# A two-layer transformer pair on one core: gather, row parts, router order and GpSimd's place in the expert stages

## The chip, the cores and the metric

The program runs on one core of a Trainium2 chip. The metric is the device time of one execution in microseconds (us); the time of a kernel is the median of its runs. Engines are called PE (TensorE), PEld (its weight loads), DVE (VectorE), ACT (ScalarE), POOL (GpSimd) and SP (SyncE, which here only issues DMAs).

## The reference, cut to what matters

256 tokens of width 1024 pass through a first block (block attention, a short convolution, two dense feed-forward parts) and a second one (a gated recurrence, a stick-breaking attention, two expert parts). The change is in the two expert parts, each of which computes this, with 4 groups of 4 experts of width 256:

```python
probs_g = softmax(xf @ w_group + b_group)              # 4 groups
p_top, g_idx = top_k(probs_g, 1)                       # every token takes one group
logits_e = (xf @ w_router + b_router).reshape(T, 4, 4)
w_top, e_local = top_k(softmax(logits_e[group]), 2)    # and two experts in it
gates = p_top * w_top / sum(w_top) at those two experts
h = silu(xf @ w_gate[e]) * (xf @ w_up[e])
y = sum over e of gates[:, e] * (h @ w_down[e])
```

All is float32. Matrix products are made of three products of parts: a float32 value is cut into a high part (a copy rounded to the type that PE multiplies at full rate) and a low part (value minus high part), and high*high, high*low and low*high are summed.

## The kernel before, in words

**Weights.** All weights are streamed in units of 1 MB (128 partitions x 2048 float32). SP loads a unit into one of 6 raw buffers, ACT writes its high part (`split`, line 678), DVE its low part (line 1347), PE multiplies with it, each engine in the same order of units, with 3 buffers of parts. A raw buffer is loaded again when both parts of its unit are written. Before a stage, `ahead` splits its first three units.

**Sorting tokens by group.** An expert stage (`moe`, once as "moe0" and once as "moe1") sorts the 256 tokens into four windows of 128 slots, one for each group, and a fifth one for what doesn't fit, so that the matrices of an expert meet one window only. In the order of time:

- After the norm, PE transposes the rows x (`after_norm`, line 2691); ACT and DVE apply the gain and bias of the norm and write the high and low part `h_high` and `h_low` in four blocks of two columns k (lines 749 and 1442).
- `router` (lines 2704 and 2705): 32 small products give the router's sums; first all eight k of token tile 0, then all of tile 1. Ahead of it and of other waits PE runs `keep_busy`: products of no use, so many calls (two instructions of the trace each) that it isn't idle.
- DVE adds biases and finds each token's group (lines 1910 to 1926); it signals `group_ready` at line 1924. PE counts tokens with triangular products (line 2729, `pos_ready`), DVE turns the counts into places and writes two selection matrices of 128 x 512 (line 1935, `sel_ready`, counted twice for each stage) into `act_high` and `act_low`.
- ACT writes the high part of the un-transposed rows (line 1135), once the router's products are done, since it lies in the same memory as `h_high`; DVE writes its low part (line 1939) into the memory of `h_low`.
- PE gathers (line 2743): for each of the 8 column blocks k, rows times selection matrix gives the transposed tokens of all four windows, 512 columns in one PSUM bank; 32 products. The banks are `GBANK`, two of them used twice. ACT takes each bank out with gain and bias (line 1143, 128 x 512) into `in_windows`, and window 0 gets its high part (line 1154, in two halves) and low part from DVE (line 2015, in two halves, `window_ready`).
- Meanwhile DVE copies the selection matrices for later use (line 1942), finds the base of the overflow group (lines 1944 to 1958), and ranks the experts (`ranks`, lines 1964 to 1975: 15 instructions of at most 40 elements), and only then comes its first half of window 0; the gates follow (`gates`, lines 1981 to 1999), then the second half.

**The expert loop.** 20 tiles c, four experts on each of the four windows and four on the fifth. `gate_up(c)`: 24 products of 512 columns (two units); in tile 0 PE also makes the gates of the slots between the two halves (`gate_in`, line 2759). ACT takes the silu (line 1160), DVE the product with the gate (line 2022), PE turns it (`turn`, line 2804), ACT and DVE write its parts (lines 1166 and 2029), and `down(c)` follows with a third unit, after `gate_up(c + 1)`. For `sel_turn` (line 2769) PE transposes the selection matrices after tile 0; `scatter` brings windows back to rows.

**GpSimd.** `apply_rows` multiplies the rows x by the norm's gain and adds its bias in place, four instructions of 128 x 1024 with a wait between any two (lines 645 and 647). They must come after the last reading of the bare rows. Before, in the expert stages, they wait for `window_ready`: both halves of window 0. After them POOL issues DMAs for later rows of constants. The rows that it writes are next read for the overflow window, after tile 2 (`over_in`, which waits for `ln_applied`).

Of the kernel before, what the change touches and what calls it, by code (L numbers as in the profile page):

```python
# [10 lines left out]
ALU = mybir.AluOpType  # L11
# [84 lines left out]
GBANK = (0, 1, 4, 5, 6, 7, 4, 5)  # L96
# [4 lines left out]
def build(nc, A, out):  # L101
    ctx = ExitStack()
    with ctx:
# [17 lines left out]
        tv = sb("rows", [P, TT, D])  # L121
        W = sb("scratch", [P, 41 * 256])
        Z = sb("small", [P, 8 * 256])
# [39 lines left out]
        rows_h, rows_l = (a[:, :, :].rearrange("p k (t s) -> p k t s", t=TT) for a in (hh, hl))  # L163
# [235 lines left out]
        def half_heads(u):  # L399

            return slice(3 * u, 3 * u + 3)

# [174 lines left out]
        def _(pool):  # L577
# [59 lines left out]
            def apply_rows(turns):  # L637
# [3 lines left out]
                if turns != 8:  # L641
                    pool.wait_ge(window_ready, 2 if turns == 7 else GRP + 4)
# [18 lines left out]
        def _(act):  # L661
# [464 lines left out]
            sp_in, rsum, rhi = Count(router_ready), Count(router_sums), Count(rows_high)  # L1126
# [4 lines left out]
            def moe(ph, scale, shift):  # L1131
                def sort_in():

                    act.wait_ge(router_sums, rsum.up())
# [6 lines left out]
                    for k in range(KT):  # L1141
                        act.wait_ge(gathered, gth.up())
                        act.activation(in_windows[:, 0:GRP, k, :], ps[:, GBANK[k], :].rearrange("p (w s) -> p w s", w=GRP),
                                       ACT.Identity, bias=shift[:, k:k + 1], scale=scale[:, k:k + 1]).then_inc(gather_taken, 1)
                        gtk.up()
# [187 lines left out]
        def _(dve):  # L1333
# [572 lines left out]
            def sort_in():  # L1906
# [21 lines left out]

                place, over = by_tile(rt[:, 304:312]), rt[:, 312:314]
# [81 lines left out]
            def moe(ph):  # L2011
# [122 lines left out]
        def _(pe):  # L2134
# [546 lines left out]
            def after_norm(count, fill):  # L2681
                keep_busy(fill, 0)
                for t in range(TT):
# [4 lines left out]
                    for g in range(4):  # L2688
# [3 lines left out]
                        if t:  # L2692
                            i.then_inc(xt_ready, 1)
                            xt.up()

            def router():

                keep_busy(8, 0)
                pe.wait_ge(rw_low, rwlr.up())
                for t in range(TT):  # L2700
                    tok = slice(t * P, (t + 1) * P)
                    for k in range(KT):
                        bank_of_h(t == 0, k)
                        pe.matmul(ps[:, 3, 40 * t:40 * t + 40], hh[:, k, tok], rwr[:, k, :], start=k == 0, stop=False, skip_group_check=True)
# [11 lines left out]
            def moe(applied):  # L2716
                first_tri, all_ones = mstrict[:, 0:P], ones[:, :]

                def sort_in():
# [3 lines left out]
                    pe.matmul(ps[:, 2, 0:P], all_ones, ident[:, :], start=False, stop=True, skip_group_check=True)  # L2723
                    pe.wait_ge(group_ready, grp.up())
# [10 lines left out]
                    for k0 in (0, 4):  # L2735
                        for part in (rows_h, rows_l):
                            if part is rows_l and k0 == 0:
                                pe.wait_ge(rows_low, rlo.up())
                            for k in range(k0, k0 + 4):
                                if part is rows_h and k >= 6:  # L2740
                                    pe.wait_ge(gather_taken, gtk.value(k - 3))
                                for t in range(TT):
                                    i = pe.matmul(ps[:, GBANK[k], :], part[:, k, t, :], sel_r[t],  # L2743
# [239 lines left out]
```

## Time and profile before

| | |
|---|---|
| median of 3 runs | 1465.17 us (1461.89 to 1466.07) |
| the profiled execution's own time | 1463.39 us |
| span of its trace | 1461.7 us |
| mean granted clock of PE, share of full | 0.971 |
| PE busy | 1367.6 us, 94% of the span |
| PEld busy | 1170.8 us, 80% |
| DVE busy | 1037.7 us, 71% |
| ACT busy | 767.4 us, 52% |
| POOL busy | 88.4 us, 6% |
| DMA | 327.72 MB, mean 224 GB/s |

The trace is of one execution. Busy shares are means over stages that have different limits; what a part of the change is worth has to be read in its own stage. A row of the timeline has the start in us from the start of the span, the duration in us of one instruction or of several in a row, the engine, the line, the operation, what it writes and reads, how many, and in brackets the idle time of the engine before it with what ended it. The first expert stage begins with the norm at about 869 us and its loop ends at about 1097; the second goes from about 1222 to 1447, some 352.7 us later.

### The profile page before, as it was taken

The page shows a single profiled execution, that of the slowest core. Times are in us where ns is not written, and L with a number is a line of the kernel's source. Part 1 is how long each engine was busy: PE and PEld are TensorE (multiplying, and loading weights), DVE is VectorE, ACT ScalarE, POOL GpSimd, SP SyncE. Part 2 cuts the span into 40 slices and gives each one's busy share as a digit, 9 for nine tenths or more (in the row PEclk, how much of TensorE's full clock was granted, in tenths as well). Part 3 has the DMA queues.
Part 4 walks back from the last instruction along what each step waited for, and adds up shares of the span by engine and source line. Part 5 has one row for each costly group of instructions (what it writes and reads, how often), then busy time and mean ns, then how long its engine had stood idle before and what let it go on. Part 6 is the DMA issues. An engine that isn't in the chain of part 4 may idle for free.

```text
span 1461.7 us, 19477 instructions
## 1 busy us (share of the span) xinstructions
PE 1367.6 (94%) x7482; PEld 1170.8 (80%) x7482; DVE 1037.7 (71%) x1057; ACT 767.4 (52%) x753; POOL 88.4 (6%) x81
## 2 busy tenths in 40 slices
PE   5996889999999999999999988999998988999995
PEld 5975778888799878888999977888878977788884
DVE  6686677788776566454665757788885465888886
ACT  2666343434433343433465345677774565577773
POOL 0010000000000000000000012200004000400000
PEclk9999899999999999999999998999998999899998
DMA  9984558999585366555553341999994413499991
GB/s 358 387 303 156 174 174 300 309 309 307 185 285 172 114 204 203 187 188 174 171 159 130 112 134 59 311 330 349 348 355 134 161 59 113 121 345 348 347 355 41
DMA packets 208909, 327.72 MB, mean 224 GB/s; under 512 B 9456, under 2 KB 146352, under 8 KB 208832
## 3 DMA queue, kind: packets, MB, share of 16 engines
q1 hardware_dynamic: 195536, 276.71, 56.5%
q0 software_dynamic: 13296, 49.93, 10.3%
q8 instruction: 54, 0.88, 0.3%
q14 instruction: 23, 0.19, 0.0%
HBM read 325.56 MB, written 1.05 MB: 223 GB/s over the span
## 4 chain that ended last, share of the span: by engine, by line
PE 79%; DVE 12%; ACT 5%; issue 2%; DMA 1%; SPq 0%; DVEq 0%; ACTq 0%
PE ps L2140 23%; PE ps L2142 22%; PE ps L2141 22%; DVE w_low L1347 3%; ACT w_high L678 2%; PE ps L2639 1%; PE ps L2837 1%; PE ps L2743 1%; PE ps L2481 1%; DMA raw<-in_w_qkv 1%; DVE stats L1861 1%; DVE h_low L2015 1%; DVE x_rows L1852 1%; DVE ps L1453 1%; PE ps L2804 1%
## 5 line engine op out<-in xcount | busy, mean ns | idle before, releaser
L1347 DVE TENSOR_TENSOR w_low<-raw,w_high 128x2048 fp32r<-128x2048 f32 x254 | 588.2, 2320 | 268.8 <-ACT w_high L678 266.7
L678 ACT ACTIVATE w_high<-raw 128x2048 fp32r<-128x2048 f32 x254 | 484.1, 1908 | 344.8 <-PE ps L2142 317.6
L2140 PE MATMUL ps<-w_high,h_high 128*128 128x512 f32 (+1 forms) x896 | 355.6, 397 | 11.4 <-DVE h_low L1442 4.0
L2142 PE MATMUL ps<-w_high,h_low 128*128 128x512 f32 (+1 forms) x896 | 348.2, 389 | 0.0
L2141 PE MATMUL ps<-w_low,h_high 128*128 128x512 f32 (+1 forms) x896 | 347.9, 388 | 0.0
L2140 PEld LDWEIGHTS ps<-w_high,h_high 128*128 128x128 f32 x896 | 170.1, 190 | 46.5 <-issue 8.2
L2142 PEld LDWEIGHTS ps<-w_high,h_low 128*128 128x128 f32 x896 | 169.6, 189 | 35.1
L2141 PEld LDWEIGHTS ps<-w_low,h_high 128*128 128x128 f32 x896 | 170.3, 190 | 32.4 <-issue 0.2
L2140 PE MATMUL ps<-h_high,w_high 128*128 128x256 f32 x592 | 172.3, 291 | 5.2 <-DVE h_low L1442 3.8
L2141 PE MATMUL ps<-h_low,w_high 128*128 128x256 f32 x592 | 169.3, 286 | 0.0
L2142 PE MATMUL ps<-h_high,w_low 128*128 128x256 f32 x592 | 169.2, 286 | 0.0
L2140 PE MATMUL ps<-w_high,act_high 128*128 128x512 f32 x336 | 133.5, 397 | 4.4 <-DVE act_low L2029 4.4
L2142 PE MATMUL ps<-w_high,act_low 128*128 128x512 f32 x336 | 131.1, 390 | 0.0
L2141 PE MATMUL ps<-w_low,act_high 128*128 128x512 f32 x336 | 130.9, 390 | 0.0
L2140 PEld LDWEIGHTS ps<-h_high,w_high 128*128 128x128 f32 x592 | 115.5, 195 | 8.9 <-issue 8.6
L2141 PEld LDWEIGHTS ps<-h_low,w_high 128*128 128x128 f32 x592 | 115.5, 195 | 0.5 <-issue 0.5
L2142 PEld LDWEIGHTS ps<-h_high,w_low 128*128 128x128 f32 x592 | 115.4, 195 | 0.0
L2140 PEld LDWEIGHTS ps<-w_high,act_high 128*128 128x128 f32 x336 | 63.1, 188 | 24.1 <-DVE act_low L2029 10.7
L2142 PEld LDWEIGHTS ps<-w_high,act_low 128*128 128x128 f32 x336 | 63.1, 188 | 13.4
L2141 PEld LDWEIGHTS ps<-w_low,act_high 128*128 128x128 f32 x336 | 63.1, 188 | 12.4
L586 POOL DMA_DIRECT2D scratch<-in_w_ada x40 | 30.2, 755 | 471.9 <-DVE scratch L1395 264.9
L1395 DVE SCALAR_TENSOR_TENSOR scratch<-scratch,silu_c 128x512 f32<-128x512 f32 x70 | 52.6, 752 | 2.5
(352 smaller groups left out, 1483.6 us busy)
## 6 DMA issues: line engine op xcount, KB each, us to landing
raw<-in_w_down SPq DMA_DIRECT2D x124, 512.0 KB, 5.0
raw<-in_w_gate_up SPq DMA_DIRECT2D x88, 512.0 KB, 5.2
scratch<-in_w_ada POOLq DMA_DIRECT2D x40, 1024.0 KB, 5.6
raw<-in_w_gate SPq DMA_DIRECT2D x80, 512.0 KB, 5.2
raw<-in_w_up SPq DMA_DIRECT2D x80, 512.0 KB, 6.8
raw<-in_w_qkv SPq DMA_DIRECT2D x24, 512.0 KB, 13.0
raw<-in_w_o SPq DMA_DIRECT2D x24, 512.0 KB, 4.8
raw<-in_w_in SPq DMA_DIRECT2D x24, 512.0 KB, 4.9
```

The costliest lines, as they stand in the source:

```text
L586: pool.dma_start(cring[:, q, :, :], v[:, q * UK:(q + 1) * UK, bass.ds(c * NC, NC)]) \
L678: act.activation(wh[u % SPL][:, :, 0:w], raw[u % RAW][:, :, 0:w], ACT.Copy).then_inc(h_split, 1)
L1347: dve.tensor_tensor(wl[u % SPL][:, :, 0:w], raw[u % RAW][:, :, 0:w], wh[u % SPL][:, :, 0:w].bitcast(F32), ALU.subtract).then_inc(l_split, 1)
L1395: i = dve.scalar_tensor_tensor(acc, w, s, acc, ALU.mult, ALU.add)
L1453: dve.tensor_scalar(b, b, scale[:, k:k + 1], shift[:, k:k + 1], ALU.mult, ALU.add).then_inc(v_ready if q else dve_step, 1)
L1852: dve.scalar_tensor_tensor(x2, x2, ALPHA, ps[:, 4 + 2 * t:6 + 2 * t, :], ALU.mult, ALU.add).then_inc(dve_step, 1)
L1861: dve.bn_stats(st[:, 32 + 12 * t + 6 * a:38 + 12 * t + 6 * a], xs[:, t, a * 512:(a + 1) * 512]).then_inc(dve_step, 1)
L2015: dve.tensor_tensor(window_h(hl, w)[:, ks, :], in_windows[:, w, ks, :], window_h(hh, w)[:, ks, :].bitcast(F32), ALU.subtract).then_inc(win ...
L2140: pe.matmul(o, h1, h2, start=start, stop=False, skip_group_check=True)
L2141: pe.matmul(o, h1, l2, start=False, stop=False, skip_group_check=True)
L2142: return pe.matmul(o, l1, h2, start=False, stop=stop, skip_group_check=True)
L2481: i = pe.transpose(ps[:, 2, k * S + t * P:k * S + (t + 1) * P], Z[:, 512 + t * FW + k * P:512 + t * FW + (k + 1) * P], ident[:, :])
```

## The change

In both expert stages:

1. The high part of the rows lies in the memory of `rows` and the low part in two pieces of `features` and `scratch`, no longer over `h_high` and `h_low`. ACT writes the high part without waiting for the router's sums. DVE writes the low part in two instructions, and ahead of its wait for PE's counts (`pos_ready`) instead of behind the selection matrices.
2. The gather is made in two halves: windows 0 and 1 for all k ahead of `gate_up(0)` (32 products of 256 columns), windows 2 and 3 (32 more) in the new `other_windows` behind `gate_up(0)`, ahead of `turn`. Each bank holds two k, and ACT takes out 128 x 256 eight times ahead of the loop and eight times after the first silu. To make room for these, the high and low part of the unit of `down(0)` are written in tile 1, ahead of that tile's own.
3. The router's products go block by block (k outside, tiles inside).
4. POOL's four instructions wait for the selection matrices (`sel_ready`), no longer for window 0.
5. More `keep_busy`: 14 calls for 10 after the norm, 3 new ones between the transposes of the two token tiles (also in the stage after moe0, which has the same function), 11 for 8 ahead of the router, 5 new ones ahead of the wait for `group_ready`.

The diff, without the declarations of memory:

```diff
@@ gpsimd, apply_rows
                 if turns != 8:
-                    pool.wait_ge(window_ready, 2 if turns == 7 else GRP + 4)
+                    pool.wait_ge(sel_ready, 2 if turns == 7 else 4)
@@ scalar, moe
+                def windows_out(w0, k):
+                    if k % 2 == 0:
+                        act.wait_ge(gathered, gth.up())
+                    act.activation(in_windows[:, w0:w0 + 2, k, :], gather_bank(k).rearrange("p (w s) -> p w s", w=2),
+                                   ACT.Identity, bias=shift[:, k:k + 1], scale=scale[:, k:k + 1]).then_inc(gather_taken, 1)
                 def sort_in():
-                    act.wait_ge(router_sums, rsum.up())
                     act.activation(rows_h, x_parts, ACT.Copy).then_inc(rows_high, 1)
...
                     for k in range(KT):
-                        act.wait_ge(gathered, gth.up())
-                        act.activation(in_windows[:, 0:GRP, k, :], ps[:, GBANK[k], :].rearrange("p (w s) -> p w s", w=GRP),
-                                       ACT.Identity, bias=shift[:, k:k + 1], scale=scale[:, k:k + 1]).then_inc(gather_taken, 1)
+                        windows_out(0, k)
...
                 split()
                 silu()
-                split(1, True)
+                for k in range(KT):
+                    windows_out(2, k)
                 n[0] += 2
                 for c in range(1, NTILE):
                     w, e = divmod(c, GRP)
                     high()
+                    if c == 1:
+                        split(-1, True)
                     split()
@@ vector, sort_in
+                dve.wait_ge(rows_high, rhi.up())
+                for i, x in enumerate(rows_l):
+                    ks = slice(UK * i, UK * i + UK)
+                    dve.tensor_tensor(x, x_parts[:, ks, :, :], rows_h[:, ks, :, :].bitcast(F32), ALU.subtract).then_inc(rows_low, 1)
+                    dve.wait_ge(rows_low, rlo.up())
                 dve.wait_ge(pos_ready, psr.up())
...
-                dve.wait_ge(rows_high, rhi.up())
-                dve.tensor_tensor(rows_l, x_parts, rows_h.bitcast(F32), ALU.subtract).then_inc(rows_low, 1)
-                dve.wait_ge(rows_low, rlo.up())
@@ vector, moe
                 product(0)
-                split(1)
                 n[0] += 2
                 for c in range(1, NTILE):
                     w, e = divmod(c, GRP)
                     low_part()
+                    if c == 1:
+                        split(-1)
                     split()
@@ tensor, after_norm, router, moe
                             xt.up()
+                    if t == 0:
+                        keep_busy(3, 0)
...
-                keep_busy(8, 0)
+                keep_busy(11, 0)
                 pe.wait_ge(rw_low, rwlr.up())
-                for t in range(TT):
-                    tok = slice(t * P, (t + 1) * P)
-                    for k in range(KT):
-                        bank_of_h(t == 0, k)
-                        pe.matmul(ps[:, 3, 40 * t:40 * t + 40], hh[:, k, tok], rwr[:, k, :], start=k == 0, ...)
+                for k in range(KT):
+                    bank_of_h(True, k)
+                    for t in range(TT):
+                        tok = slice(t * P, (t + 1) * P)
+                        pe.matmul(ps[:, 3, 40 * t:40 * t + 40], hh[:, k, tok], rwr[:, k, :], start=k == t == 0, ...)
...
+                    keep_busy(5, 0)
                     pe.wait_ge(group_ready, grp.up())
...
+                def gather(k, w0, low):
+                    part = rows_l[k // UK][:, k % UK] if low else rows_h[:, k]
+                    for t in range(TT):
+                        i = pe.matmul(gather_bank(k), part[:, t, :], sel_r[t][:, w0 * P:(w0 + 2) * P], ...)
+                    if low and k % 2:
+                        i.then_inc(gathered, 1)
+
+                def other_windows():
+                    pe.wait_ge(gather_taken, gtk.up(KT))
+                    for k in range(0, KT, 2):
+                        for low in (False, True):
+                            for j in range(2):
+                                gather(k + j, 2, low)
...
                 def sel_turn():
+                    pe.wait_ge(gather_taken, gtk.up(KT))
...
                 sort_in()
                 gate_up(0)
+                other_windows()
...
-            after_norm(5, 10)
+            after_norm(5, 14)
...
-            after_norm(7, 10)
+            after_norm(7, 14)
```

## Rows read from the trace of the kernel before

**Rows 1.** The page's chain of work that ended last, shares by engine.

```profile
PE 79%; DVE 12%; ACT 5%; issue 2%; DMA 1%; SPq 0%; DVEq 0%; ACTq 0%
```

**Rows 2.** Waits from 905 to 1100 us: waiting instruction, who ended it, total, times, longest.

```profile
ACT w_high L678 <- PE ps L2142: 29.1, 26, 3.8
```

**Rows 3.** Timeline of PE at the entry of the first expert stage.

```profile
878.17 1.95 PE L2226 MATMUL ps<-ident,ones 128*128 128x128 f32 x16
880.98 0.26 PE L2704 MATMUL ps<-router_parts,h_high 128*128 128x40 f32 x1 [0.85 <-DVE h_low L1442]
...
887.58 0.37 PE L2705 MATMUL ps<-router_parts,h_low 128*128 128x20 f32 x1
...
893.56 0.80 PE L2743 MATMUL ps<-act_high,h_high 128*128 128x512 f32 x1
...
902.33 0.40 PE L2743 MATMUL ps<-act_low,h_low 128*128 128x512 f32 x1
902.57 0.40 PE L2140 MATMUL ps<-w_high,h_high 128*128 128x512 f32 x1
...
905.67 2.41 PE L2759 MATMUL ps<-gates,scratch 128*128 128x4 f32 x20 [0.21 <-DVE h_low L2015]
...
913.09 0.69 PE L2804 MATMUL ps<-ident,small 128*128 128x128 f32 x2 [2.13 <-DVE small L2022]
...
920.42 0.39 PE L2140 MATMUL ps<-w_high,act_high 128*128 128x512 f32 x1
```

**Rows 4.** Timeline of DVE in the same stretch.

```profile
883.11 2.28 DVE L1347 TENSOR_TENSOR w_low<-raw,w_high 128x2048 fp32r<-128x2048 f32 x1
887.98 0.20 DVE L1910 TENSOR_TENSOR scratch<-ps,scratch 128x40 f32<-128x40 f32 x1 [2.59 <-PE ps L2705]
...
889.27 0.17 DVE L1924 TENSOR_TENSOR scratch<-scratch 128x8 f32<-128x8 f32 x1
...
892.82 0.69 DVE L1935 TENSOR_TENSOR act_low<-ps,scratch 128x512 fp32r<-128x512 f32 x1
...
895.87 0.43 DVE L1942 COPY scratch<-act_high 128x512 f32<-128x512 f32 x1
...
898.35 0.09 DVE L1964 MEMSET scratch<- 128x40 f32 x1
...
901.65 0.69 DVE L2015 TENSOR_TENSOR h_low<-features,h_high 128x512 fp32r<-128x512 f32 x1
...
904.93 0.69 DVE L2015 TENSOR_TENSOR h_low<-features,h_high 128x512 fp32r<-128x512 f32 x1 [0.48 <-ACT h_high L1154]
```

**Rows 5.** Timeline of ACT in the same stretch.

```profile
887.98 1.91 ACT L1135 ACTIVATE h_high<-x_rows 128x2048 fp32r<-128x2048 f32 x1 [3.82 <-PE ps L2705]
...
901.38 2.78 ACT L1143 ACTIVATE features<-ps,cols 128x512 f32<-128x512 f32 x4 [0.63 <-PE ps L2743]
```

**Rows 6.** Timeline of POOL, its instructions in the first expert stage.

```profile
905.86 4.21 POOL L645 TENSOR_TENSOR x_rows<-x_rows,scratch 128x1024 f32<-128x1024 f32 x1 [47.91 <-DVE h_low L2015]
910.15 4.29 POOL L647 TENSOR_TENSOR x_rows<-x_rows,scratch 128x1024 f32<-128x1024 f32 x1
...
918.95 2.41 POOL L647 TENSOR_TENSOR x_rows<-x_rows,scratch 128x1024 f32<-128x1024 f32 x1
```

**Rows 7.** Timeline of DVE beside those instructions of POOL.

```profile
907.74 4.48 DVE L1347 TENSOR_TENSOR w_low<-raw,w_high 128x2048 fp32r<-128x2048 f32 x1
...
912.15 0.16 DVE L2006 COPY scratch<-ps 128x16 f32<-128x16 f32 x1
...
919.91 3.59 DVE L1347 TENSOR_TENSOR w_low<-raw,w_high 128x2048 fp32r<-128x2048 f32 x1 [2.98 <-ACT w_high L678]
```

**Rows 8.** Stretches: length, busy us of PE, PEld, DVE, ACT, POOL, granted clock, DMA share, GB/s.

```profile
913.20:916.40 3.20, 3.20 (x9) 2.62 (x10) 3.19 (x1) 0.38 (x1) 3.12 (x2) 0.50 0.79 246
```

**Rows 9.** Timeline of PE in the second expert stage.

```profile
1271.83 0.39 PE L2140 MATMUL ps<-w_high,act_high 128*128 128x512 f32 x1
```

**Rows 10.** Timeline of PE in the stage after the first expert stage.

```profile
1104.65 1.97 PE L2691 MATMUL ps<-ident,x_rows 128*128 128x128 f32 x8 [0.77 <-DVE x_rows L1880]
```

More of the change, by code:

```diff
@@ L121, in build @@
         tv = sb("rows", [P, TT, D])
+        rows_at = nc.sbuf_base - TT * D * 4
+        rows_hi = nc.alloc_sbuf_tensor_at("rows_high_part", [P, KT, S], F32R, offset=rows_at)
         W = sb("scratch", [P, 41 * 256])
+        scratch_at = nc.sbuf_base - 41 * 256 * 4
+        rows_lo = [nc.alloc_sbuf_tensor_at(f"rows_low_part{i}", [P, UK, S], F32R, offset=o)
+                   for i, o in enumerate((features_at + 16 * S * 4, scratch_at + 20 * 256 * 4))]
         Z = sb("small", [P, 8 * 256])
@@ L161, in build @@
         rt = W[:, 12 * 256:20 * 256]
-        rows_h, rows_l = (a[:, :, :].rearrange("p k (t s) -> p k t s", t=TT) for a in (hh, hl))
+        rows_h = rows_hi[:, :, :].rearrange("p k (t s) -> p k t s", t=TT)
+        rows_l = [a[:, :, :].rearrange("p k (t s) -> p k t s", t=TT) for a in rows_lo]
         x_parts = xs[:, :, :].rearrange("p t (k s) -> p k t s", s=P)
@@ L401, in half_heads, with gather_bank @@
             return slice(3 * u, 3 * u + 3)
+        def gather_bank(k):
+            return ps[:, 4 + k // 2, (k % 2) * S:(k % 2 + 1) * S]
         def level_bank(l, u):
@@ L1125, in _ @@
             transposed_mod(*ln_cols(0, 0), 0)
-            sp_in, rsum, rhi = Count(router_ready), Count(router_sums), Count(rows_high)
+            sp_in, rhi = Count(router_ready), Count(rows_high)
             gth, gtk, whi = Count(gathered), Count(gather_taken), Count(window_high)
@@ L2734, in sort_in @@
                     pe.wait_ge(rows_high, rhi.up())
-                    for k0 in (0, 4):
-                        for part in (rows_h, rows_l):
-                            if part is rows_l and k0 == 0:
+                    for k0 in (0, UK):
+                        for low in (False, True):
+                            if low:
                                 pe.wait_ge(rows_low, rlo.up())
[L2739 to L2743, printed above, removed]
-                                                  start=part is rows_h and t == 0, stop=part is rows_l and t == 1, skip_group_check=True)
-                                if part is rows_l:
-                                    i.then_inc(gathered, 1)
-                                    gth.up()
-                    gtk.up(8)
+                            for k in range(k0, k0 + UK):
+                                gather(k, 0, low)
+                def gather(k, w0, low):
+                    part = rows_l[k // UK][:, k % UK] if low else rows_h[:, k]
+                    for t in range(TT):
+                        i = pe.matmul(gather_bank(k), part[:, t, :], sel_r[t][:, w0 * P:(w0 + 2) * P],
+                                      start=not low and t == 0 and k % 2 == 0, stop=low and t == 1, skip_group_check=True)
+                    if low and k % 2:
+                        i.then_inc(gathered, 1)
+                        gth.up()
+                def other_windows():
+                    pe.wait_ge(gather_taken, gtk.up(KT))
+                    for k in range(0, KT, 2):
+                        for low in (False, True):
+                            for j in range(2):
+                                gather(k + j, 2, low)
                 def gate_in():
```

5 lines of the change are left out of this document (2 added, 3 removed).

## The prediction

> **What bounds the kernel now.** I read the chain of work that ended last first: PE has 79% of it, DVE 12%, ACT 5% [rows 1]. Then the waits in the first expert loop: the weight copies of ACT wait for PE to free buffers, 29.1 us in 26 waits, and none in the list waits for a raw load [rows 2]. So the loop runs at PE's pace, and what the change can move is the time at which the loop gets under way; a microsecond won or lost ahead of tile 1 is carried to the end, twice (moe0 and moe1). So the timelines of the engines from 869 to 925 us are the view that decides. There the path is: PE's router until 887.9, slowed by a clock that has fallen to half on the way (its first product has 0.26 us, its last 0.37) [rows 3]; DVE's selection until 893.5 [rows 4]; PE's gather from 893.56 to 902.57, when `gate_up(0)` starts [rows 3]. DVE's ranks end at 901.6, and the low part of window 0 ends at 902.3 [rows 4], so DVE is as late as the gather: taking time from the gather alone brings next to nothing. Then PE idles 2.13 us ahead of `turn(0)` at 913.09, because DVE's product is late [rows 3], and after this idle time the clock is at half for 3.2 us [rows 8], which costs 1.6. `down(0)` starts at 920.42.
>
> **The router and the row parts.** A call of `keep_busy` takes 0.24 us at full clock (16 instructions, 8 calls, in 1.95) [rows 3]. The idle time of PE ahead of the router, 0.85 us [rows 3], is filled by 3 calls, that ahead of the second transposes, about the same (0.77 in the later stage) [rows 10], by 3 more; they just fit. If the clock stays full, 32 products at the pace of the fills or a little under, 0.11 us, are 3.5 us from 880.98: the router ends at about 884.5, 3.4 earlier. But DVE then still has a weight split, until 885.39 [rows 4], so its chain starts at 885.4 for 887.98. `group_ready` comes 1.46 later (887.98 to 889.44) [rows 4], at 886.9. ACT's high part of the rows, 1.91 us [rows 5], no longer waits and is done by 886.1. The low part, 2.3 us in one instruction, some 2.5 in two, now stands where DVE waited 2.2 us for the counts: from 887.1 to 889.6. PE's ten counting products, 1.1 to 2.3 us after 886.9, are hidden beside it. Place and selections take 1.7 us: done at 891.3, for 893.5 before. **Gain 2.2 us**, and no wait for the low part is left in the gather. The 5 new calls ahead of `group_ready` end at 886.3 at full clock; at half clock they would be 1.1 us late, which the low part hides.
>
> **The gather.** A product of 512 columns takes 0.24 us at full clock (902.33 to 902.57) [rows 3], so 32 of 256 columns, at 0.12, are 3.8 us: 891.3 to 895.2. ACT's takings, 0.70 for 512 columns [rows 5], so about 0.43 for 256, end near 897. By themselves they would let the loop start at 897. What holds it is DVE: from the copy at 895.87 to the window at 901.65 it has 5.8 us of work [rows 4], in the new kernel from 891.3 to 897.1, then the window's 0.7. Without GpSimd PE would start `gate_up(0)` at 897.8, 4.8 us earlier than before.
>
> **GpSimd.** Its four instructions now start at 891.5, in the middle of this work. What do they do to DVE? Beside DVE's weight splits the trace shows it: the split that was issued at 907.74 lasted 4.48 us, where an undisturbed one has 2.28 [rows 4, 7]; POOL's first instruction ended at 910.07 (905.86 + 4.21) [rows 6], and 910.07 + 2.2 is 912.2, the split's end. The one issued at 919.91 lasted 3.59 us [rows 7]: POOL's last one, which ran already, ended at 921.36 at its own pace of 2.41 [rows 6], and 921.36 + 2.2 is 923.5 again. So two instructions don't share the time; the later one stands until the other ends. And the copy from PSUM at 912.15 took 0.16 [rows 7] while POOL's second instruction was waiting or running (910.15 to 914.44) [rows 6]: an instruction that reads PSUM isn't held.
>
> This rule is also in the Trainium skill, page "SBUF — State Buffer", section "Who interferes with whom": DVE instructions with two inputs in SBUF, and copies in a two-port mode, exclude a GpSimd instruction that reads SBUF for the whole of either. It speaks against this part of the change; this case's trace agrees for large instructions, and no run here shows it yet for small ones. With shared bandwidth instead, the sum below would be that of the second rival.
>
> No row shows small DVE instructions of two SBUF inputs beside POOL. The lower bound of their cost is nothing; the upper one is four holds of 2.3 us, 9.2. The nearest rows are the held splits, of the same operation, so I take the hold for small ones too. Then: the first copy runs (891.3 to 891.7), POOL takes its turn to 894.0, the second copy, POOL to 896.6, one instruction or two, POOL to 899.1, one rank instruction, POOL to 901.5. Since POOL is back 0.08 us after each end, and DVE leaves a gap after each small instruction, they alternate. Of DVE's work only what reads one SBUF operand or PSUM goes on meanwhile, about 1.3 us. So the ranks end at 897.1 + 9.2 - 1.3 - 0.4 (its start is later than the copy) = 904.6, the window at 905.3, and PE starts `gate_up(0)` at 905.3 instead of 902.6: **2.7 us later, where 4.8 earlier was to be had.** Next in line: POOL's row constants and `ln_applied` come earlier; nobody waits for them, as `over_in` is 40 us later.
>
> PE has then been idle from about 895 to 905, and its clock will be at half at the start of `gate_up(0)`: **1.6 us** as after the idle time before `turn(0)`; between nothing and 3.
>
> **From `gate_up(0)` to `down(0)`.** First half 2.7 + 1.6, gates of the slots 2.3, second half 2.7: ends at 914.6, for 911.0. From the ranks' end DVE takes 4.0 us to the end of the window's second half (901.65 to 905.62) [rows 4]: 908.6, in time. DVE's splits, no longer held, end at about 914, and silu and product, both short, by 915.6; they are hidden beside `other_windows`, 32 x 0.12 = 3.8 us, until 918.5. `turn(0)` with 0.3, then `gate_up(1)`, 5.4 us at full clock, for 7.0 before. `down(0)` starts at 924.2, for 920.42. Its unit is split later than before: ACT's takings end 0.9 behind the gather, at 919.4, the high part of `turn` at 919.9, the unit's high part at 921.8 and low part at 924.1; that just suffices. The load behind it starts 7 us later than before, but it has six buffers' time. So **moe0 is 3.8 us slower.**
>
> **moe1.** The same instructions; the transposes come 352.7 us later, and `down(0)` at 1271.83 [rows 9] is at 919.1 in the time of moe0, since its router kept the full clock longer. The new one is bound by DVE, so it comes out as in moe0: 924.2 - 919.1 = **5.1 us slower.**
>
> **Between.** In the stage after moe0 the 3 calls fill 0.77 us ahead of transposes that took 1.97 us at half clock [rows 10], 1.09 at full. Gain up to 0.9, or 0.6 lost if the clock is low already; I take nothing.
>
> **Sum:** 3.8 + 5.1 = 8.9 us. The profiled execution had 1463.4 (span 1461.7 and 1.7 around it): 1472.3. It lies 1.8 below the median of the runs, 1465.2, to which the forecast is stated: 1474.
>
> **Rivals.**
> - *Small instructions aren't held (faster).* The hold decides the sign: if the loop start moves earlier than about 901.5, no time is lost. With all else as above, PE starts at 897.8, may lose 1.6 to the clock after an idle time of 2.6 us, and `down(0)` comes at 916.5: 3.9 less in moe0 and 2.6 less in moe1, 1465.2 - 6.5 = 1458.7. For it: all that the trace shows is held has 2048 elements. Against: POOL's own instructions stood whole behind DVE's.
> - *Only copies and the window are held (same).* The second copy waits 2.2 us, the first window half for POOL's fourth instruction, until 901.5: PE starts at 902.2 with the clock at half, +0.7 and +2.0: 1468.
> - *The clock.* It falls already in the router, as before at 882.6. Then the router ends at 887, DVE's chain is 1.5 later in each stage: with the holds 1477. Its opposite, no loss in `gate_up(0)`, gives 1471.
> - *The change doesn't do what it says:* the router is bound by `h_low`'s last block (883.2) and DVE's split; that part is counted as such above.
>
> **How the numbers follow.** The holds on all instructions: 0.62, 1474, with the clock and bounds 1470 to 1479. Only large ones: 0.14, 1468, from 1465 to 1471. None: 0.20, 1458.7, from 1455 to 1462. What is left, 0.04, is around no change. A measurement can tell 0.3%, 4.4 us, from none. Faster 0.20; same 0.16; slower 0.64. The range goes from 1460, which leaves out over half of the fast case, to 1479. The likeliest case's own is 1470 to 1479.
>
> **What would show it.** Right: in the timeline behind the selection, copies and rank instructions of 2 us and more, four of them, each ending 0.1 to 0.4 us after an instruction of POOL; the first window half near 905; an idle PE for some 8 us ahead of `gate_up(0)` and a granted clock of 0.5 in it; splits of 2.3 us everywhere in the loop; no idle time ahead of `turn(0)`. Wrong: rank instructions of 0.2 us beside POOL, and `gate_up(0)` at 898. The selection at 893 instead of 891.3 would say that the router kept its half clock.

## The result, and the profile after

The changed kernel takes 1473.1 us (median of 5 runs, 1471.8 to 1475.6); the kernel before 1462.4 in the runs beside it. The ratio is 1.0063, with a 95% interval of 1.0048 to 1.0079: **slower by 0.6%**, some 9 us. The forecast was 1474, slower, stated to a kernel before of 1465.2, which is 0.6% too. The span of the profiled execution is 1471.5 us, 9.8 more than before.

The page after: PE's share of the chain fell from 79% to 77%, DVE's rose from 12% to 13% [rows 1].

```profile
PE 1369.7 (93%) x7612; PEld 1177.8 (80%) x7612; DVE 1043.1 (71%) x1059; ACT 771.2 (52%) x769; POOL 77.1 (5%) x81
...
PE 77%; DVE 13%; ACT 6%; issue 2%; DMA 1%; SPq 0%; DVEq 0%; ACTq 0%
```

The timeline of POOL in the first expert stage, for [rows 6]. Its instructions are almost at their own pace now (2.34 us), and the first two at 2.45:

```profile
891.26 2.46 POOL L654 TENSOR_TENSOR x_rows<-x_rows,scratch 128x1024 f32<-128x1024 f32 x1 [33.61 <-DVE act_low L1956]
893.80 2.45 POOL L656 TENSOR_TENSOR x_rows<-x_rows,scratch 128x1024 f32<-128x1024 f32 x1
896.33 2.35 POOL L654 TENSOR_TENSOR x_rows<-x_rows,scratch 128x1024 f32<-128x1024 f32 x1
898.76 2.34 POOL L656 TENSOR_TENSOR x_rows<-x_rows,scratch 128x1024 f32<-128x1024 f32 x1
```

The timeline of DVE in the same stretch, for [rows 4]:

```profile
885.17 0.19 DVE L1926 TENSOR_TENSOR scratch<-ps,scratch 128x40 f32<-128x40 f32 x1
...
886.89 2.48 DVE L1948 TENSOR_TENSOR rows_low_part<-x_rows,rows_high_part 128x1024 fp32r<-128x1024 f32 x2
...
890.33 0.69 DVE L1956 TENSOR_TENSOR act_low<-ps,scratch 128x512 fp32r<-128x512 f32 x1
891.05 0.43 DVE L1960 COPY scratch<-act_high 128x512 f32<-128x512 f32 x1
891.51 2.49 DVE L1960 COPY scratch<-act_low 128x512 f32<-128x512 f32 x1
...
894.24 2.04 DVE L1964 TENSOR_SCALAR scratch<-scratch 128x2 f32<-128x2 f32 x1
896.32 0.42 DVE L1966 TENSOR_TENSOR scratch<-ps,scratch 128x256 f32<-128x256 f32 x1
...
896.97 1.73 DVE L1972 TENSOR_TENSOR scratch<-scratch,group_ids 128x4 f32<-128x4 f32 x1
...
898.92 0.15 DVE L1976 CAST over_base<-scratch 128x1 int32<-128x1 f32 x1
...
899.16 1.99 DVE L1986 TENSOR_TENSOR scratch<-scratch 128x40 f32<-128x40 f32 x1
901.19 0.20 DVE L1988 TENSOR_TENSOR scratch<-scratch 128x40 f32<-128x40 f32 x1
...
904.12 0.69 DVE L2033 TENSOR_TENSOR h_low<-features,h_high 128x512 fp32r<-128x512 f32 x1
```

The same four instructions in the kernel before, with nothing of POOL beside them (timeline of DVE):

```profile
896.33 0.43 DVE L1942 COPY scratch<-act_low 128x512 f32<-128x512 f32 x1
...
896.99 0.17 DVE L1946 TENSOR_SCALAR scratch<-scratch 128x2 f32<-128x2 f32 x1
...
897.85 0.16 DVE L1954 TENSOR_TENSOR scratch<-scratch,group_ids 128x4 f32<-128x4 f32 x1
...
898.47 0.20 DVE L1968 TENSOR_TENSOR scratch<-scratch 128x40 f32<-128x40 f32 x1
```

Put them side by side. Four instructions of DVE that have 0.43, 0.17, 0.16 and 0.20 us by themselves last 2.49, 2.04, 1.73 and 1.99; the first copy ended at 891.48, POOL's instructions end at 893.72, 896.25, 898.68 and 901.10, and each of the four long ones ends 0.02 to 0.3 us behind one of these. The excess is 2.06 + 1.87 + 1.57 + 1.79 = 7.3 us. What reads PSUM (the 0.42 at 896.32) runs through. In the second expert stage the same four have the same 2.49, 2.04, 1.73 and 1.99.

The timeline of PE, for [rows 3]:

```profile
884.29 0.26 PE L2726 MATMUL ps<-router_parts,h_low 128*128 128x20 f32 x1
...
891.08 0.58 PE L2768 MATMUL ps<-act_high,rows_high_part 128*128 128x256 f32 x1 [0.19 <-DVE act_low L1956]
...
904.87 0.80 PE L2159 MATMUL ps<-w_high,h_high 128*128 128x512 f32 x1 [9.15 <-DVE h_low L2033]
...
909.82 2.30 PE L2791 MATMUL ps<-gates,scratch 128*128 128x4 f32 x20
...
920.23 0.38 PE L2837 MATMUL ps<-ident,small 128*128 128x128 f32 x2
...
926.00 0.47 PE L2159 MATMUL ps<-w_high,act_high 128*128 128x512 f32 x1
```

PE idles 9.15 us ahead of `gate_up(0)`, which starts 2.3 us later than before, and runs at half clock twice in it, as these stretches show (columns as in [rows 8]):

```profile
905.00:909.00 4.00, 4.00 (x10) 3.13 (x11) 3.69 (x11) 0.00 (x0) 0.00 (x0) 0.50 0.24 80
...
913.00:917.00 4.00, 4.00 (x15) 3.18 (x15) 1.58 (x3) 0.38 (x1) 0.00 (x0) 0.60 0.65 217
```

**Where the time went.** PE's timeline can be cut at four points: the first transposes of each norm (f), the transposes of `turn(1)` (line 2804 before), and the same in the second stage. For example, before: f is 875.37 and `turn(1)` 924.24, so the entry of the first stage is 48.87 us. From `turn(1)` on, the tiles take the same time in nearly all kernels, to 0.1 us (8.42, 12.45, 8.42, 10.41 and so on).

```
us                     entry 1   tiles+norm   between   entry 2   tiles to end
before                   48.9       178.6      125.3      47.6       186.1
after                    54.7       178.5      122.9      54.1       186.2
```

The two entries lost 5.8 and 6.5 us, 12.3 together; the stage between them is 2.5 shorter; the rest is equal. 12.3 - 2.5 = 9.8, the difference of the spans.

### The profile page after: what moved, and what is told of

It is laid out like the page before. It is cut to its first block, busy times and chain, and to the rows that moved or that the text cites. A ratio compares the mean times of both kernels' runs of the same rounds, so it can differ in the third digit from the quotient of the medians.

```text
span 1471.5 us, 19755 instructions
## 1 busy us (share of the span) xinstructions
PE 1369.7 (93%) x7612; PEld 1177.8 (80%) x7612; DVE 1043.1 (71%) x1059; ACT 771.2 (52%) x769; POOL 77.1 (5%) x81
## 4 chain that ended last, share of the span: by engine, by line
PE 77%; DVE 13%; ACT 6%; issue 2%; DMA 1%; SPq 0%; DVEq 0%; ACTq 0%
PE ps L2159 23%; PE ps L2161 22%; PE ps L2160 22%; DVE w_low L1363 3%; ACT w_high L687 2%; PE ps L2658 1%; PE ps L2870 1%; PE ps L2500 1%; DMA raw<-in_w_qkv 1%; DVE h_low L2033 1%; DVE stats L1877 1%; DVE x_rows L1868 1%; DVE ps L1469 1%; PE ps L2768 1%; DVE scratch L1411 1%
## 5 line engine op out<-in xcount | busy, mean ns | idle before, releaser
L1363 DVE TENSOR_TENSOR w_low<-raw,w_high 128x2048 fp32r<-128x2048 f32 x254 | 578.8, 2282 | 271.7 <-ACT w_high L687 269.7
## 6 DMA issues: line engine op xcount, KB each, us to landing
raw<-in_w_qkv SPq DMA_DIRECT2D x24, 512.0 KB, 12.3
```

What stands on the lines that cost most here:

```text
L1363: dve.tensor_tensor(wl[u % SPL][:, :, 0:w], raw[u % RAW][:, :, 0:w], wh[u % SPL][:, :, 0:w].bitcast(F32), ALU.subtract).then_inc(l_split, 1)
```

## The experiments

The table has all kernels in the same cut, one profiled execution each, with the ratio to the kernel before and its interval. The runs of one kernel lie 3.5 to 8 us apart (e5: 1459.6 to 1467.7), so a difference of 1 or 2 us in a column is one of two executions, and tells of the kernels only where the timeline shows its cause.

```
                     ratio (95%)              entry 1  tiles+norm  between  entry 2  to end
e1_pool_back         0.9944 (0.9928-0.9959)     45.4     178.5      122.7     44.9    186.0
e2_pool_alone        1.0087 (1.0073-1.0101)     56.2     178.6      125.0     54.8    186.1
e3_pool_narrow       0.9933 (0.9915-0.9952)     45.4     178.5      125.5     43.6    186.0
e4_router_fills      0.9939 (0.9923-0.9955)     44.7     178.6      122.4     45.3    186.2
e5_fill_transposes   0.9993 (0.9982-1.0003)     48.9     178.5      125.2     47.6    186.1
e6_full_gather       0.9959 (0.9943-0.9975)     47.3     180.2      122.5     47.0    186.2
e7_fill_turn         0.9937 (0.9918-0.9955)     43.8     180.1      122.2     45.3    186.2
e8_fill_turn_pool    0.9954 (0.9936-0.9972)     43.5     181.1      125.1     45.3    188.6
e9_fill_gather       0.9957 (0.9944-0.9971)     45.4     178.5      122.6     46.6    186.1
e10_three_gathers    0.9922 (0.9909-0.9936)     45.2     178.5      122.8     43.2    186.2
e11_pool_write       0.9941 (0.9922-0.9960)     48.2     178.6      122.9     46.3    186.1
e12_split_back       0.9917 (0.9902-0.9932)     43.5     180.0      122.9     41.9    186.1
```

My theory was that DVE's instructions of two inputs in memory, small ones too, are held behind GpSimd's; the main rival, that the loss comes from the gather in two halves and the late split, and GpSimd only changes places.

### e1: GpSimd back in its place, all else of the change kept

```diff
-                    pool.wait_ge(sel_ready, 2 if turns == 7 else 4)
+                    pool.wait_ge(window_ready, 2 if turns == 7 else GRP + 4)
```

> The changed kernel with part 4 undone: GpSimd's four instructions wait for window 0 again, all other parts stay. Theory (DVE's small instructions are held behind GpSimd's): DVE's ranks end near 897 instead of 904, gate_up(0) starts near 898 instead of 904.9 in the first expert stage, and down(0) comes at about 917 to 918 instead of 926.0. Twice 8 us or so: about 1457 us (1454 to 1460), faster than the kernel before by 0.2 to 0.5%. Rival (the loss comes from the gather in two halves and the late split for down(0), GpSimd only changes places): the time stays at 1470 or more.

Measured: 1456.4 us, ratio 0.9944. The timeline of PE in e1 has `gate_up(0)` 22.35 us after f (877.45), where the change has 29.6, and `turn(0)` at 35.7 for 45.0:

```profile
899.80 0.50 PE L2159 MATMUL ps<-w_high,h_high 128*128 128x512 f32 x1 [0.21 <-DVE h_low L2033]
...
913.16 0.38 PE L2837 MATMUL ps<-ident,small 128*128 128x128 f32 x2
```

One line takes the change from 0.6% slower to 0.6% faster; the ratio of the two ratios is 0.9944 / 1.0063 = 0.988, 17 us. The rival falls.

### e2: GpSimd's move alone, on the kernel before

```diff
-                    pool.wait_ge(window_ready, 2 if turns == 7 else GRP + 4)
+                    pool.wait_ge(rows_low, 1 if turns == 7 else 2)
```

> The kernel before with GpSimd's move alone: its four instructions wait for the low part of the rows (the earliest place that is allowed there, since they overwrite what it reads). Theory: of four holds of 2.3 us, 7.5 us are seen by the ranks, which end near 909 instead of 901.6; gate_up(0) starts near 910, partly with half a clock; the weight splits are no longer held, so up to 2.7 us come back. Plus 5 to 8 us for each stage: about 1475 us (1471 to 1479). Rival (small instructions are not held, the other parts cost the time): 1462, within 2.

Measured: 1478.8 us, ratio 1.0087 (the whole change: 1.0063; the two intervals overlap a little). The entries are 7.3 us longer each than in the kernel before. The same four holds stand in DVE's timeline:

```profile
897.49 2.50 DVE L1942 COPY scratch<-act_low 128x512 f32<-128x512 f32 x1
...
900.22 2.05 DVE L1946 TENSOR_SCALAR scratch<-scratch 128x2 f32<-128x2 f32 x1
...
902.95 1.75 DVE L1954 TENSOR_TENSOR scratch<-scratch,group_ids 128x4 f32<-128x4 f32 x1
...
905.17 2.00 DVE L1968 TENSOR_TENSOR scratch<-scratch 128x40 f32<-128x40 f32 x1
```

### e3: narrow instructions on GpSimd

```diff
-                    pool.tensor_tensor(xs[:, t, :], xs[:, t, :], lnv[:, 0, :], ALU.mult)...
+                    pool.tensor_tensor(xs[:, t, 0:16], xs[:, t, 0:16], lnv[:, 0, 0:16], ALU.mult)...
```

> The changed kernel, but in the expert stages GpSimd multiplies and adds in 16 of the 1024 columns only (the norm's gain and bias are left out of the other 1008 of the rows). Theory: the hold lasts as long as GpSimd's instruction, so hardly any is left: copies 0.43 and small instructions 0.2 us, gate_up(0) near 898, and later splits are free too: about 1456 us (1453 to 1459). Rival (what delays DVE is that the two engines alternate, whatever the instructions' size): still above 1468.

Measured: 1456.7 us, ratio 0.9933. The place is that of the change, only the size is different: POOL's first instruction has 0.30 us, DVE's second copy its own 0.43 and the first rank instruction 0.20. First e3's timeline of POOL, then that of DVE:

```profile
893.36 0.30 POOL L655 TENSOR_TENSOR x_rows<-x_rows,scratch 128x16 f32<-128x16 f32 x1 [33.45 <-DVE act_low L1957]
```

```profile
893.61 0.43 DVE L1961 COPY scratch<-act_low 128x512 f32<-128x512 f32 x1
...
895.76 0.20 DVE L1987 TENSOR_TENSOR scratch<-scratch 128x40 f32<-128x40 f32 x1
```

So it isn't the taking of turns that costs, but how long the holder holds. e3 and e1 also agree with each other: in its old place GpSimd's work costs the rest of the change nothing in the first entry (45.4 both), and 1.3 us in the second, where PE waits for the held split of `down(0)`.

### e4: router by blocks and fills, on the kernel before

The diff is that of parts 3 and 5 of the change.

> The kernel before with parts 3 and 5 alone: router block by block, and the additional keep_busy. Theory: the router ends at 884.4 instead of 887.9, DVE's selection starts at once after its split, 2.6 us earlier in the first expert stage and 1.2 in the second, and all behind it keeps its distance since DVE's chain and the gather both start with it: 1459 us (1457 to 1461), 0.1 to 0.3% faster. Rival (the fills only move the clock's fall to another place): 1462, within 2.

Measured: 1456.4 us, ratio 0.9939, 9 us for the 3.5 expected, so outside the range that I gave. The mechanism is as told: the entries are 4.2 and 2.3 us shorter. The gain in the first one is larger than the 2.6 by which DVE's selection starts earlier, because PE's counts there now run at full clock too and DVE waits less for them (1.21 us for 2.22; in the second stage still 2.10). Another 2.9 us of the profiled execution are in the stage between (see e5). **These two parts are all that the change gains**: e1, with every part but GpSimd's, isn't faster than e4. How much is the router's order and how much the fills, no run separates.

### e5: the three fills between the transposes, alone

```diff
                         if t:
                             i.then_inc(xt_ready, 1)
                             xt.up()
+                    if t == 0:
+                        keep_busy(3, 0)
```

> The kernel before with three calls of keep_busy between the transposes of the two token tiles and nothing else. In the changed kernel and in the first experiments the stage between the two expert stages is 2.4 to 2.9 us shorter than in the kernel before, which my forecast had put at nothing. Theory: these three calls alone do it, since PE's clock no longer falls ahead of the second transposes; 1462.5 us for 1465.2 (ratio 0.998, 0.997 to 0.999), with the first product of that stage's weights at full clock sooner. Rival (it comes from something else, for example from the earlier start of the expert stage): no change, ratio 1.000.

Measured: ratio 0.9993, interval 0.9982 to 1.0003, which leaves room for a gain of 0.2% at most; in the trace, of the slowest of its 12 runs, the stage between takes 125.2, as before. So the three fills don't shorten it by themselves. Over the traces this stage has two values: about 125.3 (before, e2, e3, e5, e8) and 122.7 (all others). Three of the first have the three fills (e3, e5, e8), but so have all of the second, so the fills may still be needed for the shorter value. What goes with the value is the clock: in all five with the longer stage it falls some 80 us into the stage, among the short products of the stick-breaking attention, and stays low longer at its beginning; in the others it doesn't. Here are the rows of busy time by stretch at the same place of the code, 6 us each, of the kernel before (granted clock 0.72) and then of the changed one (1.00), with the columns of [rows 8]:

```profile
1186.00:1192.00 6.00, 5.60 (x30) 4.52 (x32) 2.95 (x5) 4.69 (x7) 0.00 (x0) 0.72 0.00 0
```

```profile
1190.00:1196.00 6.00, 5.32 (x41) 4.37 (x42) 4.32 (x7) 5.75 (x9) 0.00 (x0) 1.00 0.01 3
```

What decides it I have not shown. The fills are the only edit in that stage, and with them both values occur; since each trace is of one execution, I can't say either whether the value belongs to the kernel or changes from run to run.

### e6: the gather undone in e1

Full width for all four windows ahead of `gate_up(0)`, nothing behind it, the split for `down(0)` in its old place:

```diff
-                gate_up(0)
-                other_windows()
+                gate_up(0)
...
-                    if c == 1:
-                        split(-1, True)
```

> The experiment e1 (GpSimd back in its place) with the gather undone as well: all four windows ahead of gate_up(0), and the unit of down(0) split in its old place; the row parts stay in their new memory and order. Theory: the gather again ends after DVE's ranks, gate_up(0) starts 2 to 3 us later than in e1, but no PE work stands between gate_up(0) and turn(0), where PE again idles and its clock falls; so 1 to 3 us more than e1: ratio to the kernel before 0.995 to 0.997. Rival (the gather's halves are worth the 4.8 us that I gave to the loop start in the forecast): ratio 1.000 or above. Rival (they are worth nothing or cost): 0.9944 or less.

Measured: ratio 0.9959, entries 1.8 and 2.1 us longer than in e1. So with the low part of the rows ahead of the selection, the halves are worth 2 us in each stage: not the 4.8 by which the loop could start earlier, since 3.8 us of products come back behind `gate_up(0)`, where PE had 2.1 us of idle time for them. And e6 is slower than e4 (47.3 for 44.7 in the first entry), which has the full gather too, but the rows' parts in the old order: with PE's counts done sooner, DVE has only 1.2 us to wait for them (e4), no longer 2.2, and the 2.5 us of low part push the selection matrices, and with them a full gather, back by 1.3. The row parts' new order and the half gather need each other, and together they bring nothing over e4.

### e7 and e8: fills ahead of `turn(0)`, and GpSimd later

e7 is e4 with:

```diff
                 for c in range(NTILE):
+                    if c == 0:
+                        keep_busy(9, 1)
                     turn()
```

> The experiment e4 (router by blocks and fills on the kernel before) with nine more calls of keep_busy ahead of turn(0), in the 2.15 us in which PE waits for the product. Theory: the clock no longer falls in gate_up(1), 1.5 us won in each expert stage: ratio to the kernel before 0.992 (e4 had 0.9939). Rival (the clock falls all the same, somewhat later, or the fills delay turn(0)): 0.994 or more.

Measured: 0.9937, which can't be told from e4's 0.9939. The first entry is 0.9 us shorter, and the clock now falls at the end of the first loop instead (tiles+norm 180.1). The second is the same, since there was nothing to win: PE waits only 1.07 us ahead of `turn(0)` there in e4, and the clock falls in `gate_up(0)`, in e4 and in e7, not in `gate_up(1)`. That the clock doesn't fall in `gate_up(1)` of the first stage is shown; that it brings time on the whole is not.

e8 is e7 with GpSimd behind the product of tile 0:

```diff
-                    pool.wait_ge(window_ready, 2 if turns == 7 else GRP + 4)
+                    pool.wait_ge(act_ready, 4 * NFF + 1 if turns == 7 else 4 * NFF + NTILE + 1)
```

> e7 with GpSimd's four instructions behind the first tile's product on DVE (5 us later than in the kernel before, instead of 12 earlier as in the change). Theory: DVE's two weight splits ahead of that product are no longer held, so turn(0) comes 1.1 us earlier; the holds fall on the splits for down(0) and gate_up(2), which have 2 us or more to spare. The fills now are about 1 us too many. Ratio 0.990 to 0.992. Rival (a held split for down(0) stops PE, as it did for 1.25 us in the second stage of e1): 0.993 or more.

Measured: 0.9954, an interval (0.9936 to 0.9972) that overlaps e7's. By the trace the rival holds, one tile later than I put it: three of GpSimd's instructions alternate with weight splits (4.3 us each), DVE falls behind, and PE waits ahead of `down(1)`, as the timeline of PE in e8 shows:

```profile
926.43 0.50 PE L2140 MATMUL ps<-w_high,act_high 128*128 128x512 f32 x1 [1.73 <-DVE act_low L2029]
```

Tile 1 takes 10.9 us for 8.4 in both stages. A later place for GpSimd isn't free either: it costs 2.5 us in each stage of this trace, and the entries gain 0.4 us at most. The times alone don't settle it, since another 2.9 us between the traces of e8 and e7 lie in the stage between.

### e9, e10 and e12: more of the gather under DVE's ranks

e9 is e1 with `keep_busy(12, 0)` for `keep_busy(4, 0)` ahead of the gather.

> The experiment e1 (all of the change but GpSimd's move) with 12 calls of keep_busy instead of 4 between PE's counts and the gather, where it idles 2.1 us in the first expert stage and 1.2 in the second. Theory: the clock no longer falls in the gather; but DVE's ranks, not the gather, set the start of gate_up(0), so little is won, up to 1 us for each stage: ratio to the kernel before 0.993 to 0.9945 (e1: 0.9944). Rival (the gather is the bound, and the full clock brings its 2 us to the loop): 0.991 to 0.992.

Measured: 0.9957 (0.9944 to 0.9971), no gain over e1's 0.9944, and outside the 0.993 to 0.9945 that I gave. The gather is not the bound, as the theory had it: at full clock it only makes PE wait longer for DVE's ranks (2.42 us), and in the second stage the clock then falls in `gate_up(0)` (entry 46.6 for 44.9).

e10 uses the time of that wait. Of windows 2 and 3 the first four k are gathered there, into banks 1 and 2:

```diff
+                    pe.wait_ge(over_ready, applied // 2 + 1)
+                    for k in (0, 2):
+                        for low in (False, True):
+                            for j in range(2):
+                                gather(k + j, 2, low, early_bank(k + j))
...
-                    for k in range(0, KT, 2):
+                    for k in (4, 6):
```

> e9 with the second half of the gather divided again: of windows 2 and 3 the columns k 0 to 3 are gathered ahead of gate_up(0), while PE waits for DVE's ranks, into two banks that are free until turn(0) and down(0); only k 4 to 7 stay behind gate_up(0), 1.9 us, which is about what PE waits for the product there. In e1 all of it, 3.8 us, stood there. Theory: turn(0) comes 1.9 us or more earlier in each stage: ratio 0.989 to 0.992, faster than every kernel so far. Rival (DVE's splits, held behind GpSimd, then set the product and turn(0)): 0.993 or more.

Measured: 0.9922 (0.9909 to 0.9936), just outside the range of the theory. `turn(0)` comes 33.8 and 32.3 us after f, for 35.7 and 33.9 in e1. But then, in the first stage, PE waits for the split of `down(0)`, in the timeline of PE in e10:

```profile
916.47 0.47 PE L2165 MATMUL ps<-w_high,act_high 128*128 128x512 f32 x1 [1.63 <-DVE w_low L1369]
```

e12 puts that split back to its old place:

```diff
                 silu()
-                for k in range(4, KT):
+                split(1, True)
+                for k in range(4, KT):
...
-                    if c == 1:
-                        split(-1, True)
```

> e10 with the unit of down(0) split in its old place, behind the first silu and product; with only four takings left there is room. In e10 PE waits 1.63 us for the low part of that unit ahead of down(0), since it comes behind turn(0) and is then held by GpSimd's last instruction. Theory: this wait goes, 1.1 to 1.7 us in each stage: ratio to the kernel before 0.989 to 0.991 (e10: 0.9922). Rival (the four takings and the copy of turn(0) behind the split now come late and stop PE instead): 0.992 or more, with a wait for the low part of the activations ahead of down(0).

Measured: 1451.1 us, ratio 0.9917 (0.9902 to 0.9932), outside the 0.989 to 0.991 that I gave, and not to be told from e10's by the times. In the trace the wait is gone and the entries are 43.5 and 41.9, by 1.3 to 1.7 shorter than e10's; 1.5 of that went again to a fallen clock at the end of the first loop. **e12 is faster than the kernel before by 0.8% and than the changed kernel by 1.5%** (0.9917 / 1.0063).

### e11: GpSimd only writes

```diff
-                    pool.tensor_tensor(xs[:, t, :], xs[:, t, :], lnv[:, 0, :], ALU.mult)...
+                    pool.memset(xs[:, t, :], 0.0)...
```

> The changed kernel, but GpSimd's four instructions in each expert stage only write (zeros in place of the rows, so the residual and the overflow window lose their input); each should last about 0.9 us, from 1.39 for 1536 columns in the kernel before. Theory (the hold is of what both engines read): copies at two elements a cycle may still be held for up to 0.9 us, small instructions with two inputs in memory are not held at all, 0.2 us each: ratio to the kernel before 0.993 to 0.996, as e3. Rival (any instruction of GpSimd holds them): four holds of 0.9 us, ratio 0.997 or more, and four small instructions of about 0.8 us in the trace.

Measured: 0.9941. First the last two instructions in e11's timeline of POOL in the first stage, then the timeline of DVE beside the four:

```profile
894.70 0.95 POOL L655 MEMSET x_rows<- 128x1024 f32 x1
895.71 0.95 POOL L657 MEMSET x_rows<- 128x1024 f32 x1
```

```profile
892.61 1.14 DVE L1966 COPY scratch<-act_low 128x512 f32<-128x512 f32 x1
...
893.98 0.68 DVE L1970 TENSOR_SCALAR scratch<-scratch 128x2 f32<-128x2 f32 x1
...
895.35 0.16 DVE L1978 TENSOR_TENSOR scratch<-scratch,group_ids 128x4 f32<-128x4 f32 x1
...
895.98 0.20 DVE L1992 TENSOR_TENSOR scratch<-scratch 128x40 f32<-128x40 f32 x1
```

The copy and the TENSOR_SCALAR are still held. The other two that the change holds run in the middle of a memset (894.70 to 895.65 and 895.71 to 896.66) in their own 0.16 and 0.20 us, and so they do in the second stage. So there are two kinds of hold: instructions of two inputs in memory are held only while GpSimd reads; copies and scalar operations from memory to memory by its writes too. The Trainium skill, page "SBUF — State Buffer", section "Who interferes with whom", makes this same division, and by it the second kind is in a two-port mode; the trace agrees for these four instructions, and shows that two columns are enough for it. The entries are 2.8 and 1.4 us longer than e1's all the same: the two holds that are left make 1.2 of it, and in the first stage the clock then is at half for 3.4 us in the first half of `gate_up(0)`.

## Why the prediction was right, and where it wasn't

**The router and the selection: right.** The router ended at 884.5, DVE's chain started at 885.2, the selection was done at 891.0; forecast 884.5, 885.4 and 891.3. The idle times were filled, to 0.18 us. The clock still fell, at 885.5, behind the router with PE busy, and was at half until 892.3, through the counts; DVE's low part of the rows hid it, as the prediction had said for such a case.

**The holds: right,** the step on which the sign hung. Four holds, one for each instruction of GpSimd, 7.3 us against 7.5; the ranks ended at 904.1 against 904.6, and `gate_up(0)` started at 904.9 against 905.3. e1, e2, e3 and e11 show the mechanism from four sides: taken away, made alone, made short, made of another kind. The division of kinds was incomplete. I let what reads one operand in memory go on, but the TENSOR_SCALAR 128x2 reads one, and it was one of the four, with 1.87 us; and I held instructions of two inputs and copies for the same case, which e11 separates.

**The clock: under-sized.** I took 1.6 us of loss once, and 3 at most. It was at half twice, until 909.4 in the first half of `gate_up(0)` and from 912.8 to 916.2 in the second, 4.5 us and 3.4 us of it. With the gates of the slots `gate_up(0)` took 11.5 us (904.9 to 916.4) where the sum has 9.3, so the loss was some 3.8. `down(0)` came at 926.0 for 924.2, and the first stage lost 5.8 us for 3.8, the second 6.5 for 5.1.

**The stage between: I took nothing, it gave 2.5 back.** By e5 the three fills alone don't do it; what goes with it is whether the clock falls there, and why it does is open. So that the sum, 8.9 against 9.8, came so near is luck in part: 3.4 us too little in the entries and 2.5 too much between them cancelled for the most part. The entries alone would have given 12.3.

**What the other parts are worth** was told with its sign, but not its place: router and fills alone bring 0.6% (e4, I had 3.5 us for them in its expectation), the gather in halves and the rows' parts, to which I gave the earlier loop start, bring nothing on top of them (e1 against e4).

## What to carry to other kernels

Before an elementwise instruction of GpSimd is moved to a "quiet" place, look at what DVE does there, in number of instructions and not in busy time: a chain of 0.2 us instructions from memory to memory, each waiting for the last, pays the whole rest of GpSimd's instruction every time the two meet, 7.3 us here for four meetings. Where DVE has slack behind a buffer, as with weight splits, the same meetings cost less: nothing and 1.3 us in the two stages of e1, but 2.5 in each of e8, so the slack has to be read there too. And a wait of PE for such a chain is room for products that can be brought forward (e10), while moving them behind the wait only helps as far as PE idles there.

## What the runs showed of the hardware

- A hold doesn't depend on the size of the held: 4 columns waited 1.57 us, 2 columns 1.87 us, 512 columns 2.06 us. It depends on the holder's: 16 columns on GpSimd left nothing of it (e3).
- Which small instructions run through, in the changed kernel: inputs in PSUM (0.42 and 0.16 at 896.3 and 896.8), and the CAST to int32 of one column from memory to memory, 0.15 us at 898.92, in the middle of GpSimd's fourth (898.76 to 901.10).
- PE's clock fell not only after idle time. In the first stage of the change and of e1, e2, e3, e6, e9, e10, e11 and e12 it fell during the second half of `gate_up(0)` with PE busy; what stood ahead of it were the gates' 20 products of 4 columns, 2.3 us. In the kernel before, e4 and e5, with the same products, it fell there only after the 2.1 us of idle time ahead of `turn(0)`, and in e7 and e8, which have that time filled, not at all.
- The same wait may be followed by a fall or not: e6, e7 and e12 have 1.5 us more at the end of the first loop, where the clock falls behind a wait of PE of 2.0 us; the other eleven kernels have the same wait, with no fall. Such falls, and 2.5 us in the stage between, are of the size of what the fills win; only the cut by stages told them apart from the edits.
